# A ring of prompt expert rows cut from three buffers to two, and a table load moved ahead of the late gathers

## The chip, the cores and the metric

The kernel runs on one core of one Trainium2 chip. The metric is the device time of one launch in microseconds; the trace is that of one profiled execution. TensorE does the matrix products, VectorE and ScalarE the elementwise work, GpSimd (POOL in the profile) issues gathers and some loads, and SyncE (SP) streams the weights.

## The reference: two layers of a hybrid backbone

128 context tokens (the prompt) and 512 latent tokens run through two layers. Each layer has four token mixers side by side, a gated merge of them with an output projection, and then an expert layer (PEER). All is float32. What matters here is the expert layer, cut to its core:

```
qry = (hc @ w_query).reshape(-1, PEER_HEADS, 2, PEER_DK // 2)
s = einsum('thpk,hpnk->thpn', qry, sub_keys)          # 8 heads x 2 tables x 128 keys
...                                                    # top 16 of 16 x 16 sums -> e, softmax -> g
act = gelu(einsum('thkd,td->thk', u_tab[e], hc))
y = einsum('thk,thkd->td', g * act, v_tab[e])
```

Each token picks 8 x 16 = 128 experts. For one of these 128 places, the u and v rows of 128 tokens are 128 rows of 2048 floats, 1 MB, fetched by one indirect DMA (a gather). Below, "row i" is the gather of place i for all 128 prompt tokens.

## The kernel before

The prompt's work is one stage ahead of the latent tokens' work, so the prompt's 128 expert rows of layer l are handled while the latent tokens of layer l go through their mixers. Every engine has its own program, written out in order, and they meet at semaphores. For the latent tokens of a layer the order is: projections for convolution and pooling; the query/key stage (16 units of four-chunk projections on TensorE, `L1980`, each with a square on ScalarE, a norm on VectorE, `L1508` to `L1539`, and transposes back on TensorE, `L2019`); pool projections (`L2038`); attention in 48 jobs; the merge stage (32 steps of a gate product `L2129` and a branch product `L2134`); the output and query projections and the scores against the sub-keys; then the latent tokens' own expert rows.

The prompt's rows are spread over this. Rows 0 to 15 (`EARLY = 16`) go with the query/key stage, one to a step: in step n VectorE does the reduction for unit n, the norm of unit n-1, the dot of row n-1 (`L1397`) and the addition of row n-2 to the accumulator (`L1407`). ScalarE makes the weight of a row between its dot and its addition. Rows 16 to 111 go with the merge stage, three to a step, and the rest with the two stages behind it.

GpSimd issues the gathers. The early rows use a ring of three buffers in `arena`; the gather of row i waits until the addition of row i-3 is done (`p_acc`). Behind the sixteenth addition GpSimd issues the loads of the windows of v (`L638`) and the bias loads, which the later two thirds of attention need. Rows 16 and up use a ring of four other buffers (`L664`); they wait for the end of attention (`o_ready`). The latent tokens' sub-keys `sk` (1 MB, `L663`), used by the scores behind the merge stage, are loaded between rows 23 and 24, since the accumulator of the early rows `yacc0` lies in the same place until row 16 is added.

Weights come in chunks of 0.5 MB through a ring of six; a chunk's place is loaded again once TensorE is through with it. In the query/key stage four units use the same four chunks, and they come free during the fourth unit.

The lines that set the order on VectorE in the query/key stage:

```
for n in range(NQ + 1):
    if n < NQ:
        qk_mean(n)
    if n >= 1:
        qk_norm(n - 1)
        prompt_rows(l, (n - 1,))
    ...
prompt_add(l, EARLY - 1)
```

Of the kernel before, what the change touches and what calls it, by code (L numbers as in the profile page):

```python
# [15 lines left out]
D = 1024  # L16
# [19 lines left out]
PAIRS = HEADS * TOPK  # L36
# [197 lines left out]
NP = 4  # L234
EARLY = 16
# [36 lines left out]
def need(eng, s, n):  # L272

    if n > 0:
        eng.wait_ge(s, n)


def backbone(nc, xT, cT, w, ada, small, rowg, lamrow, clay, poolw, subk, rope, edge, mask, bias, ckn, ckd,
             cvn, cvd, experts, y_prompt, y_sample, o_nk, o_nv, o_dk, o_dv):
    with ExitStack() as cx:  # L280
# [3 lines left out]
        def sem(name):  # L284
            return cx.enter_context(nc.semaphore(name))
# [6 lines left out]
        arena = sb("arena", [P, 28800])  # L292
# [20 lines left out]
        peidx = sb("peidx", [P, PAIRS], U32)  # L313
# [3 lines left out]
        def at(tensor, start, *shape):  # L317
            n = int(np.prod(shape))
            v = tensor[:, start:start + n]
            if len(shape) == 1:  # L320
                return v
            names = "abcd"[:len(shape)]
            return v.rearrange(f"p ({' '.join(names)}) -> p {' '.join(names)}", **dict(zip(names, shape)))
# [22 lines left out]
        sk = at(arena, 26752, 16, NKEYS)  # L346
# [10 lines left out]
        def routing(tensor, base):  # L357
# [33 lines left out]
        plamx = at(T, 1280, 2, 64)  # L391

        prow = [at(arena, a, 2 * D) for a in (16512, 18560, 10368, 14464)]
        prow0 = [at(arena, a, 2 * D) for a in (20096, 22144, 24704)]
        yacc0, yacc = at(arena, 27392, D), at(arena, 22656, D)
        pdots, pgel, pwcol = at(T, 2048, PAIRS), at(T, 2176, PAIRS), at(T, 2304, PAIRS)

        w_load = [sem(f"w_load{i}") for i in range(RING)]
# [14 lines left out]
        p_half, p_gate, p_br, p_merged, p_subk = [sem(n) for n in ("p_half", "p_gate", "p_br", "p_merged", "p_subk")]  # L413
        p_idx, p_top, p_gexp, p_gok = sem("p_idx"), sem("p_top"), sem("p_gexp"), sem("p_gok")
        p_row = [sem(f"p_row{i}") for i in range(NP)]
        p_row0 = [sem(f"p_row0{i}") for i in range(3)]
        p_dot, p_w, p_acc = sem("p_dot"), sem("p_w"), sem("p_acc")

        x_ready, sq_ready, root, h_ready = sem("x_ready"), sem("sq_ready"), sem("root"), sem("h_ready")
# [1 line left out]
        ctx_in, subk_in, u_zero, u_ready, conv_done, pool_d = [  # L421
            sem(n) for n in ("ctx_in", "subk_in", "u_zero", "u_ready", "conv_done", "pool_d")]
# [52 lines left out]
                eng.wait_ge(turn[key[0]], TURN[key] + 1)  # L475

        def row_of(i):
            return prow0[i % 3] if i < EARLY else prow[i % NP]

        def weight_of(i):  # L480
            return stp[:, i:i + 1] if i < EARLY else pwcol[:, i:i + 1]
# [4 lines left out]
        def pause(eng):  # L486

            eng.nop(nofuse=True)
# [34 lines left out]
        def _(gp):  # L523
# [77 lines left out]
            for l in range(DEPTH):  # L601
                need(gp, x_ready, l)
                for t in range(NL):
                    gp.tensor_tensor(sq[:, t], x_sb[:, t], x_sb[:, t], ALU.mult).then_inc(sq_ready, 1)
                gp.wait_ge(h_ready, 24 * l + KD)
                pause(gp)
                gp.memset(U, 0.0).then_inc(u_zero, 1)
                own.link(gp.memset(at(bsb, 0, 3, PADDED), 0.0))
                gp.dma_start(dkT[:, :, LAT:TOK], ckd[l]).then_inc(ctx_in, 16)
                gp.dma_start(nkT[:, :, LAT:TOK], ckn[l]).then_inc(ctx_in, 16)  # L610
                gp.dma_start(dv[:, NL, :], cvd[l]).then_inc(ctx_in, 16)
                gp.dma_start(nvc, cvn[l]).then_inc(ctx_in, 16)
                work = [at(bsb, i * PADDED, PADDED) for i in range(3)]
                for g, win in enumerate(POOL_WINDOWS):
                    wait_freed(gp, ("L", l, f"pl{g}"))
                    pause(gp)
                    own.link(gp.tensor_copy(work[0][:, PAD:PAD + LAT], yT[:, g, :]))
                    for means in pool_means(*work, LAT, g, win):
                        pass
                    gp.tensor_tensor(yT[:, g, :], means[:, PAD:PAD + LAT], work[0][:, PAD:PAD + LAT], ALU.subtract).then_inc(pool_d, 1)  # L620
                    gp.wait_ge(pool_d, 4 * l + g + 1)

                for i in range(2):
                    gp.wait_ge(vb_out[i], 32 * (l + 1))
                gp.wait_ge(p_idx, 2 * l + 1)
                for i in range(EARLY):
                    if i >= 3:
                        gp.wait_ge(p_acc, l * PAIRS + i - 2)
                    pause(gp)
                    gp.indirect_dma_start(row_of(i), None, experts,  # L630
                                          bass.IndirectOffsetOnAxis(ap=peidx[:, i:i + 1], axis=0)).then_inc(p_row0[i % 3], 16)
                gp.wait_ge(p_acc, l * PAIRS + EARLY)
                pause(gp)
                vg = vscr.rearrange("(r c) n -> r c n", c=GRID_W)
                for j in range(NJ):
                    for half in range(2):
                        for r in range(4):
                            gp.dma_start(vwin[32 * r:32 * r + 32, 2 * j + half, :],  # L638
                                         vg[4 * half + r, COL0[j]:COL0[j] + KB, :]).then_inc(vb_in, 16)

                for h in range(8):
                    if h >= 2:

                        gp.wait_ge(m_ready, l * NMAPS + MAP0[NDIFF + NL * (h - 1)])
                    pause(gp)
                    bh = at(bsb, (h % 2) * 1024, NJ, ROWS * KB)
                    gp.dma_start(bh, bias[l * 8 + h]).then_inc(bias_in[h % 2], 16)
                    gp.wait_ge(bias_in[h % 2], (l * 4 + (h // 2 + 1)) * 16)
                    pause(gp)
                    for j in range(NJ):  # L650
                        b3 = bh[:, j, :].rearrange("p (r k) -> p r k", k=KB)
                        gp.tensor_tensor(b3, b3, mk[:, j:j + 1, :].broadcast_to([P, ROWS, KB]), ALU.add).then_inc(bias_ok, 1)

                gp.wait_ge(o_ready, NJOBS * (l + 1))
                gp.wait_ge(p_idx, 2 * (l + 1))
                for i in range(EARLY, PAIRS):
                    if i >= EARLY + NP:
                        gp.wait_ge(p_acc, l * PAIRS + i - NP + 1)
                    if i == EARLY + 3:
                        gp.wait_ge(y_diff, 4 * (l + 1))  # L660
                    if i == EARLY + 8:
                        pause(gp)
                        gp.dma_start(sk, subk[l]).then_inc(subk_in, 16)  # L663
                    gp.indirect_dma_start(row_of(i), None, experts,  # L664
                                          bass.IndirectOffsetOnAxis(ap=peidx[:, i:i + 1], axis=0)).then_inc(p_row[i % NP], 16)

                mixer = prompt_mixer(l + 1) if l + 1 < DEPTH else iter(())
                step = None
                for t in range(NL):
                    for i in range(PAIRS):  # L670
                        n = (l * NL + t) * PAIRS + i
                        here = t * PAIRS + i
                        if i % GP == 0:
                            gp.wait_ge(idx_ready, (l * NL + t) * 2 + i // GP + 1)
                        if here == 1:
                            gp.wait_ge(p_acc, PAIRS * (l + 1))
                        if here == 7:
                            wait_unit(gp, ("E", l, "ynP"))
                        if n >= NS:
                            gp.wait_ge(v_done, n - NS + 1)  # L680
                        gp.indirect_dma_start(rows[:, n % NS, :], None, experts,  # L681
                                              bass.IndirectOffsetOnAxis(ap=eidx[:, t % 2, i:i + 1], axis=0)).then_inc(row_in[n % NS], 16)
                        if here == PAIRS:
                            wait_unit(gp, ("C", l, "s15"))
                            step = next(mixer, None)
                        elif step is not None and here >= gather_of(step) + 10:
                            step = next(mixer, None)
                assert step is None and next(mixer, None) is None
# [422 lines left out]
        def _(v):  # L1111
# [274 lines left out]
            def prompt_dot(l, i):  # L1386

                if i < EARLY:
                    v.wait_ge(p_row0[i % 3], (l * ((EARLY + 2 - i % 3) // 3) + i // 3 + 1) * 16)
                else:  # L1390
                    v.wait_ge(p_row[i % NP], (l * ((PAIRS - EARLY) // NP) + (i - EARLY) // NP + 1) * 16)
                if i == 0:
                    for name in ("hna", "hnb"):
                        wait_freed(v, ("P", l, name))
                e = row_of(i)[:, 0:D]
                d = stp[:, i:i + 1] if i < EARLY else pdots[:, i:i + 1]
                v.tensor_tensor_reduce(e, e, htok(NL), 1.0, 0.0, ALU.mult, ALU.add, d).then_inc(p_dot, 1)  # L1397
# [27 lines left out]
            for l in range(DEPTH):  # L1425
# [192 lines left out]
                for s in range(32):  # L1618
                    dp, i, dd = s // 8, s % 8 // 2, s % 2
# [725 lines left out]
```

## Time and profile before

| what | value |
|---|---|
| median of 3 runs | 5128.01 us (5121.45 to 5134.9) |
| profiled execution | 5121.45 us, span 5119.6 us |
| TensorE busy | 4417.8 us, 86% |
| VectorE busy | 3388.3 us, 66% |
| ScalarE busy | 1951.3 us, 38% |
| GpSimd busy | 1661.8 us, 32% |
| HBM read | 1667.33 MB, 327 GB/s over the span |

Busy shares are means over stages that differ: the kernel has stages in which the DMA engines are nearly full and others in which they are idle more than half of the time. A stage has to be read by itself.

### The profile page before, as it was taken

Reading aid. Unit: us, or ns where it says so; the run is one execution under the profiler, and the core shown is the slowest. Engines: PE = TensorE matmul, PEld = TensorE weight load, DVE = VectorE, ACT = ScalarE, POOL = GpSimd, SP = SyncE. Lnnn points to the kernel's source line nnn. Section 1 sums busy time; section 2 is a strip of 40 time slices with the busy share of each in tenths; the row PEclk is TensorE's granted clock in tenths of the full one; section 3 lists DMA queues with packets and bytes.
Section 4 is the critical chain, followed back from the end, with each engine's and each line's share of the span. In section 5 each row is a group of like instructions: output and inputs, shape, how many; then the busy total and the mean of one; then the engine's idle time right before and its main releaser. Section 6 shows DMA issues by size and latency. Waiting matters only on the chain.

```text
span 5119.6 us, 46892 instructions
## 1 busy us (share of the span) xinstructions
PE 4417.8 (86%) x14388; PEld 2284.2 (45%) x14388; DVE 3388.3 (66%) x7266; ACT 1951.3 (38%) x5074; POOL 1661.8 (32%) x1600
## 2 busy tenths in 40 slices
PE   7889888998899888888888898999889987777777
PEld 4674455434645333344544444644464632222222
DVE  4239865777787677775444896777778767576544
ACT  1210543343233434565533035544323433333333
POOL 3003121223244453433332322132224444434332
PEclk8899989999999999999999998999999999999999
DMA  7752526999799999999999143199979999999998
GB/s 286 252 192 79 191 78 249 350 345 351 305 420 420 420 420 411 413 394 418 405 419 419 60 140 124 61 356 356 360 279 420 412 419 422 422 421 419 421 421 353
DMA packets 277115, 1677.27 MB, mean 328 GB/s; under 512 B 31808, under 2 KB 31856, under 8 KB 112384
## 3 DMA queue, kind: packets, MB, share of 16 engines
q0 software_dynamic: 190896, 1365.43, 66.0%
q1 hardware_dynamic: 82944, 302.03, 16.1%
q10 hardware_dynamic: 3024, 6.82, 0.3%
q8 instruction: 115, 1.88, 0.1%
q14 instruction: 136, 1.11, 0.1%
HBM read 1667.33 MB, written 6.82 MB: 327 GB/s over the span
## 4 chain that ended last, share of the span: by engine, by line
DMA 39%; PE 31%; DVE 17%; ACT 7%; issue 5%; POOL 0%; SPq 0%; DVEq 0%; ACTq 0%; POOLq 0%
DMA arena<-experts,bsb 27%; PE ps L2218 12%; DMA arena<-experts,peidx 10%; PE ps L1805 5%; DVE arena L1496 4%; DVE arena L1708 3%; PE ps L1913 2%; PE ps L1980 2%; DMA wring<-w 2%; DVE arena L1407 2%; PE ps L2070 2%; PE ps L2092 2%; PE ps L1781 1%; ACT L1066 1%; ACT T L1070 1%
## 5 line engine op out<-in xcount | busy, mean ns | idle before, releaser
L2218 PE MATMUL ps<-arena,T 128*128 128x512 f32 x4096 | 1967.6, 614 | 445.2 <-ACT T L1070 444.6
L1708 DVE CUSTOM_DVE_ANT_0 arena<-arena,h_sb 128x1024 f32<-128x1024 f32 x1024 | 1252.8, 1227 | 865.0 <-DMA arena<-experts,bsb 861.4
L681 POOL DMA_INDIRECT arena<-experts,bsb x1024 | 1095.8, 1070 | 1741.4 <-PE ps L2218 1582.2
L2218 PEld LDWEIGHTS ps<-arena,T 128*128 128x128 f32 x4096 | 726.1, 192 | 1569.5 <-ACT T L1070 951.7
L1066 ACT ACTIVATE bsb<-T 128x1 f32<-128x1 f32 x1024 | 205.9, 201 | 1303.0 <-DVE T L1708 1301.3
L1805 PE MATMUL ps<-h_sb,wring 128*128 128x256 f32 (+2 forms) x2304 | 517.8, 382 | 35.1 <-DVE h_sb L1447 13.7
L2129 PE MATMUL ps<-h_sb,wring 128*128 128x512 f32 x1024 | 457.6, 600 | 33.5 <-DVE arena L1633 31.0
L1805 PEld LDWEIGHTS ps<-h_sb,wring 128*128 128x128 f32 x2304 | 380.7, 196 | 183.8 <-issue 152.0
L664 POOL DMA_INDIRECT arena<-experts,peidx x224 | 249.5, 1114 | 655.6 <-DVE arena L1407 582.1
L1070 ACT ACTIVATE T<-ident,bsb 128x128 f32<-128x128 f32 x1024 | 410.9, 401 | 33.5
L1397 DVE CUSTOM_DVE_ANT_0 arena<-arena,h_sb 128x1024 f32<-128x1024 f32 x256 | 312.7, 1222 | 113.7 <-DMA arena<-experts,peidx 112.6
L1980 PE MATMUL ps<-wring,h_sb 128*128 128x512 f32 x768 | 338.2, 598 | 0.0
L2129 PEld LDWEIGHTS ps<-h_sb,wring 128*128 128x128 f32 x1024 | 192.6, 191 | 294.3 <-issue 228.1
L1067 ACT ACTIVATE bsb<-bsb,T 128x1 f32<-128x1 f32 x1024 | 301.4, 294 | 33.2
L1407 DVE SCALAR_TENSOR_TENSOR arena<-arena,T 128x1024 f32<-128x1024 f32 x224 | 287.0, 1281 | 0.5 <-ACT T L845 0.5
L2134 PE MATMUL ps<-arena,wring 128*128 128x512 f32 x512 | 230.2, 593 | 0.0
L1980 PEld LDWEIGHTS ps<-wring,h_sb 128*128 128x128 f32 x768 | 146.2, 193 | 175.3 <-issue 175.3
L844 ACT ACTIVATE T<-T 128x1 f32<-128x1 f32 x224 | 45.3, 202 | 444.0 <-DVE T L1397 444.0
L1496 DVE SCALAR_TENSOR_TENSOR arena<-arena,sm 128x512 f32<-128x512 f32 x240 | 184.9, 849 | 0.0
L1805 PE MATMUL ps<-arena,wring 128*128 128x256 f32 (+1 forms) x768 | 150.4, 353 | 25.8 <-DVEq L1639 25.0
L2070 PE MATMUL ps<-arena 64*128 64x128 f32 (+2 forms) x512 | 151.8, 433 | 17.3 <-ACT T L961 15.2
L630 POOL DMA_INDIRECT arena<-experts,peidx x32 | 64.9, 2029 | 284.4 <-DVE arena L1407 171.6
(326 smaller groups left out, 4543.1 us busy)
## 6 DMA issues: line engine op xcount, KB each, us to landing
wring<-w SPq DMA_DIRECT2D x576, 512.0 KB, 6.2
arena<-experts,bsb POOLq DMA_INDIRECT x1024, 15.3
bsb<-bias POOLq DMA_DIRECT2D x16, 512.0 KB, 3.8
arena<-subk POOLq DMA_DIRECT2D x4, 1024.0 KB, 8.3
arena<-experts,peidx POOLq DMA_INDIRECT x256, 8.0
arena<-v_scratch POOLq DMA_DIRECT2D x64, 64.0 KB, 2.0
x_sb<-xT POOLq DMA_DIRECT2D x1, 2048.0 KB, 14.1
v_scratch<-arena ACTq DMA_DIRECT2D x8, 256.0 KB, 2.0
```

The source lines that it names most:

```text
L681: gp.indirect_dma_start(rows[:, n % NS, :], None, experts, bass.IndirectOffsetOnAxis(ap=eidx[:, t % 2, i:i + 1], axis=0)).then_inc(row_in[ ...
L1066: own.link(act.activation(gel[:, i:i + 1], dots[:, t % 2, i:i + 1], ACT.Gelu))
L1067: own.link(act.activation(wcol[:, i:i + 1], gel[:, i:i + 1], ACT.Copy, scale=gate[:, t % 2, i:i + 1]))
L1070: act.activation(diag[:, n % ND, :], ident[:], ACT.Copy, scale=wcol[:, i:i + 1]).then_inc(diag_ok, 1)
L1397: v.tensor_tensor_reduce(e, e, htok(NL), 1.0, 0.0, ALU.mult, ALU.add, d).then_inc(p_dot, 1)
L1407: v.scalar_tensor_tensor(yacc0 if i < EARLY else yacc, row, weight_of(i), yacc0 if i <= EARLY else yacc, ALU.mult, ALU.add).then_inc(p_acc, 1)
L1496: op = v.scalar_tensor_tensor(acc[:, c, :], U[:, c, 1 + k:1 + k + LAT], S(col), acc[:, c, :], ALU.mult, ALU.add)
L1708: v.tensor_tensor_reduce(e, e, htok(t), 1.0, 0.0, ALU.mult, ALU.add, dots[:, t % 2, i:i + 1]).then_inc(dot, 1)
L1805: mm = pe.matmul(bank(key, cols), chunk_of(s, l, c)[:, k * P:(k + 1) * P], src(k), start=(k == 0), stop=(k == KD - 1))
L1980: mm = pe.matmul(bank(key), h_sb[:, t, k, :], chunk_of("L", l, c0 + q)[:, kk * 512:(kk + 1) * 512], start=(k == 0), stop=(k == KD - 1))
L2129: mm = pe.matmul(ps[:, s % 2, :], chunk_of("L", l, c)[:, k * P:(k + 1) * P], h_in(k), start=(k == 0), stop=(k == KD - 1))
L2218: mm = pe.matmul(ps[:, 6 + half, :], diag[:, n % ND, :], rows[:, n % NS, D + half * 512:D + (half + 1) * 512], start=(i == 0), stop=(i == ...
```

## The change

The early ring has two buffers instead of three: the gather of row i waits for the addition of row i-2. The place that comes free takes the early accumulator, so that it no longer lies in the sub-keys' place; and the sub-keys of the latent tokens are loaded right after attention, ahead of row 16's gather, no longer between rows 23 and 24. The semaphores of the ring are numbered to match.

```
-        prow0 = [at(arena, a, 2 * D) for a in (20096, 22144, 24704)]
-        yacc0, yacc = at(arena, 27392, D), at(arena, 22656, D)
+        prow0 = [at(arena, a, 2 * D) for a in (20096, 22144)]
+        yacc0, yacc = at(arena, 25728, D), at(arena, 22656, D)
...
-        p_row0 = [sem(f"p_row0{i}") for i in range(3)]
+        p_row0 = [sem(f"p_row0{i}") for i in range(2)]
...
         def row_of(i):
-            return prow0[i % 3] if i < EARLY else prow[i % NP]
+            return prow0[i % 2] if i < EARLY else prow[i % NP]
...
                 for i in range(EARLY):
-                    if i >= 3:
-                        gp.wait_ge(p_acc, l * PAIRS + i - 2)
+                    if i >= 2:
+                        gp.wait_ge(p_acc, l * PAIRS + i - 1)
                     pause(gp)
...
                 gp.wait_ge(o_ready, NJOBS * (l + 1))
+                pause(gp)
+                gp.dma_start(sk, subk[l]).then_inc(subk_in, 16)
                 gp.wait_ge(p_idx, 2 * (l + 1))
                 for i in range(EARLY, PAIRS):
...
-                    if i == EARLY + 8:
-                        pause(gp)
-                        gp.dma_start(sk, subk[l]).then_inc(subk_in, 16)
...
-                    v.wait_ge(p_row0[i % 3], (l * ((EARLY + 2 - i % 3) // 3) + i // 3 + 1) * 16)
+                    v.wait_ge(p_row0[i % 2], (l * (EARLY // 2) + i // 2 + 1) * 16)
```

## Rows read from the trace of the kernel before

**Rows 1.** The page: chain by line, and the early gathers among the costliest groups.
```profile
DMA arena<-experts,bsb 27%; PE ps L2218 12%; DMA arena<-experts,peidx 10%; PE ps L1805 5%; DVE arena L1496 4%; DVE arena L1708 3%; PE ps L1913 2%; PE ps L1980 2%; DMA wring<-w 2%; DVE arena L1407 2%; PE ps L2070 2%; PE ps L2092 2%; PE ps L1781 1%; ACT L1066 1%; ACT T L1070 1%
...
L630 POOL DMA_INDIRECT arena<-experts,peidx x32 | 64.9, 2029 | 284.4 <-DVE arena L1407 171.6
```

**Rows 2.** Windows: length; PE, PEld, DVE, ACT, POOL busy; PEclk; DMA share; GB/s.
```profile
504.00:640.00 136.00, 120.19 (x315) 55.50 (x313) 112.34 (x204) 68.37 (x113) 32.61 (x16) 0.96 0.51 180
...
930.00:1260.00 330.00, 300.56 (x743) 141.68 (x742) 245.99 (x318) 134.12 (x263) 97.84 (x87) 0.97 0.93 351
```

**Rows 3.** Timeline of POOL, query/key stage of the first layer: start, length, instruction, idle before.
```profile
537.60 0.94 POOL L630 DMA_INDIRECT arena<-experts,peidx  x1 [12.06 <-DVE arena L1404]
548.58 0.94 POOL L630 DMA_INDIRECT arena<-experts,peidx  x1 [10.04 <-DVE arena L1407]
555.88 0.94 POOL L630 DMA_INDIRECT arena<-experts,peidx  x1 [6.37 <-DVE arena L1407]
...
570.49 0.94 POOL L630 DMA_INDIRECT arena<-experts,peidx  x1 [6.36 <-DVE arena L1407]
583.38 0.94 POOL L630 DMA_INDIRECT arena<-experts,peidx  x1 [11.96 <-DVE arena L1407]
590.46 0.94 POOL L630 DMA_INDIRECT arena<-experts,peidx  x1 [6.14 <-DVE arena L1407]
595.16 0.94 POOL L630 DMA_INDIRECT arena<-experts,peidx  x1 [3.76 <-DVE arena L1407]
602.11 0.94 POOL L630 DMA_INDIRECT arena<-experts,peidx  x1 [6.01 <-DVE arena L1407]
609.41 0.94 POOL L630 DMA_INDIRECT arena<-experts,peidx  x1 [6.37 <-DVE arena L1407]
619.42 0.94 POOL L630 DMA_INDIRECT arena<-experts,peidx  x1 [9.07 <-DVE arena L1407]
629.71 0.94 POOL L630 DMA_INDIRECT arena<-experts,peidx  x1 [9.35 <-DVE arena L1407]
634.77 0.94 POOL L630 DMA_INDIRECT arena<-experts,peidx  x1 [4.12 <-DVE arena L1407]
```

**Rows 4.** Timeline of DVE: after an addition, a dot, and attention's first reduction.
```profile
547.72 0.68 DVE L1508 TENSOR_REDUCE st<-T 128x8 f32<-128x512 f32 x1
...
552.68 1.22 DVE L1397 CUSTOM_DVE_ANT_0 arena<-arena,h_sb 128x1024 f32<-128x1024 f32 x1
...
653.92 0.82 DVE L1584 TENSOR_REDUCE st<-ps 128x1 f32<-128x640 f32 x1 [5.64 <-PE ps L2070]
```

**Rows 5.** L630 alone, windows 540 to 650, then 537 to 540, then 629 to 631.
```profile
  DVE arena L1407: 85.9, 12
...
DMA to landing us min/median/max: 5.4/5.6/8.9
...
DMA to landing us min/median/max: 9.0/9.0/9.0
...
DMA to landing us min/median/max: 7.3/7.3/7.3
```

**Rows 6.** Timeline of PE: a unit after a long wait, and one without.
```profile
529.18 1.12 PE L2019 MATMUL ps<-ident,T 128*128 128x128 f32 x4 [10.24 <-DVE T L1539]
530.09 9.14 PE L1980 MATMUL ps<-wring,h_sb 128*128 128x512 f32 x16
...
546.81 7.03 PE L1980 MATMUL ps<-wring,h_sb 128*128 128x512 f32 x16
```

**Rows 7.** Timelines of POOL and DVE around the merge stage's start.
```profile
856.43 1.00 POOL L664 DMA_INDIRECT arena<-experts,peidx  x1 [21.05 <-PE ps L2092]
...
895.91 0.57 POOL L663 DMA_DIRECT2D arena<-subk  x1 [0.95 <-DVE arena L1407]
...
878.33 1.22 DVE L1397 CUSTOM_DVE_ANT_0 arena<-arena,h_sb 128x1024 f32<-128x1024 f32 x1
...
907.30 1.23 DVE L1397 CUSTOM_DVE_ANT_0 arena<-arena,h_sb 128x1024 f32<-128x1024 f32 x1 [4.45 <-DMA arena<-experts,peidx]
```

More of the change, by code:

```diff
@@ L626, in _ @@
                 for i in range(EARLY):
-                    if i >= 3:
-                        gp.wait_ge(p_acc, l * PAIRS + i - 2)
+                    if i >= 2:
+                        gp.wait_ge(p_acc, l * PAIRS + i - 1)
                     pause(gp)
                     gp.indirect_dma_start(row_of(i), None, experts,
-                                          bass.IndirectOffsetOnAxis(ap=peidx[:, i:i + 1], axis=0)).then_inc(p_row0[i % 3], 16)
+                                          bass.IndirectOffsetOnAxis(ap=peidx[:, i:i + 1], axis=0)).then_inc(p_row0[i % 2], 16)
                 gp.wait_ge(p_acc, l * PAIRS + EARLY)
```

## The prediction

> **What bounds the kernel now.** I read the page first, then the windows, then the timelines of GpSimd, VectorE and TensorE around the two places that the diff touches, then the time from issue to landing of single gathers. On the page the reader sees that the chain that ended last is mostly gathers of expert rows, and that the early prompt gathers (L630) do not carry it; it runs through L1980, the projections beside them [rows 1]. So the early rows are now hidden, and the question is by how much. The windows show two different stages: the query/key stage (504 to 640 us) has TensorE busy 120 of 136 us with the DMA engines at 51%, while the merge stage (930 to 1260 us) has them at 93%, 351 GB/s, with TensorE busy 301 of 330 us [rows 2]. In the first stage latency counts, in the second bytes.
>
> In the query/key stage VectorE does, per step, a reduction, the norm of one unit, the dot of row i and the addition of row i-1. The page's idle time of L630, 171.6 us over 24 gathers, is twice the 85.9 us over 12 gathers of the first layer, so the second layer repeats the first [rows 1, 5].
>
> **The early ring, three buffers to two.** Today gather i waits for the addition of row i-3; after the change it waits for that of row i-2. The addition of row i-2 is the last thing in step i-1, and the dot of row i comes in the very next step. The latency, which now spreads over two steps, must fit into one.
>
> Its pieces: an addition ends at 547.72 and the next gather issues at 548.58, 0.86 us [rows 3, 4]. Landing takes 5.4 to 5.6 us from issue where no weights are moving [rows 5]; I take 5.5. From the dot's start (552.68) to the end of the addition behind it is 2.34 us: that addition released the gather at 555.88, less 0.86 is 555.02 [rows 3, 4]. Together one row cannot take less than 0.86 + 5.5 + 2.34 = 8.7 us. Today a row takes 7.30 us in this stage, seen as the distance between gathers, and TensorE's unit and its transposes take the same [rows 3, 6]. With three buffers the latency is spread over two steps and hidden.
>
> Where weights move at the same time (the ring reloads after each fourth unit), landing took 9.0 us at 537.6, 7.3 at 629.7 and up to 8.9 between [rows 5]; such a row takes 0.86 + 9.0 + 2.34 = 12.2 us or, with 7.3, 10.5.
>
> Twelve steps lie between the gathers at 537.60 and 634.77, 97.2 us: 11.0, 7.3, 7.3, 7.3, 12.9, 7.1, 4.7, 6.9, 7.3, 10.0, 10.3, 5.1 [rows 3] (the row at 563.19, between two of 7.3, isn't shown). After the change:
> Steps 2, 3, 6, 7, 9 and 10 are quiet rows: 6 x 8.7 = 52.2.
> Steps 1 and 8 meet the weights: 12.2 + 12.1. Step 1 already waits for TensorE's unit now, and that hides the first part of it.
> Step 4 begins with the reload; between 5.5 and 7.3 I take 6.4, thus 9.6. Step 12 is in the reload, 10.5.
> Steps 5 and 11 hold the convolution's centring and its norm, which keep VectorE and ScalarE busy longer than a gather takes: 12.9 and 10.3 as now.
> Sum 119.8, so 22.6 us more. A thirteenth step stands before the last norm. It waits today for ScalarE, which has the convolution's activation to do first; from the other rows that hold more than the usual work I put it at 9 us, and at the same after: nothing. That puts the end of row 13's addition at 634.77 - 0.86 + 9 = 642.9 now.
>
> Then what is late: the last norm releases TensorE's last transposes, the pool projections and the first scores of attention, all in a row. Row 15 on VectorE is not on that path: its gather waits for row 13's addition, and it is done 8.7 us and one addition of 1.2 us later, 9.9 us behind 642.9, where the first reduction of attention is at 653.92 [rows 4], 11.0 us behind. So its wait is just hidden and I count it at nothing; a gather that meets weights there costs up to 2.4 us. The window loads of v and the bias loads on GpSimd are behind the last early row too; they are needed by the sixteen-jobs-later part of attention, tens of us on, and cost nothing. Attention and all behind it start 22.6 us later, in each layer: +45.2 us. Nothing behind it works ahead of it, since each stage reads what the last one left, so nothing gives it back.
>
> The floor: all landings at 5.4 and no meeting with weights gives nine rows of 8.6, 11.0, 12.9 and 10.3, sum 111.6, +14.4 a layer. The ceiling: 9.0 also in step 4, 12 and 13 gives about +30 a layer.
>
> The Trainium skill (DMA: Bandwidth & Descriptors, "Anatomy of one DMA — SWDGE (gpsimd) path") fits a GpSimd DMA as 2.0 us and bytes over 436 GB/s. For the 1 MB of a gather that is 4.4 us, an estimate from that page, and a quiet row would take 7.6 us and hardly lose anything. The trace does not agree: twelve gathers took 5.4 us at the least [rows 5], and the measurement decides.
>
> **The load of the sub-keys moved ahead of the late gathers.** It is 1.05 MB on GpSimd's own queue. Today it issues at 895.91 with row 24's gather right behind it, and the dot that needs this gather then waits 4.45 us [rows 7]. After the change it issues as soon as attention is over, ahead of rows 16 to 18. Today row 16's gather issues at 856.43 and its dot starts at 878.33, released by VectorE's own order (four reciprocals) and not by a DMA [rows 7], so 3 us of delay to these rows are covered; were they not, the gain would be given back. The merge stage loses 1.05 MB of transfer at 351 GB/s, 3.0 us, and with the DMA at 93% [rows 2] I take it whole: -6.0 us in both layers. The bounds are 0 and the 4.45 us wait, so 0 to -9 us. The extra instruction that lets the load start, and its 0.57 us of issue [rows 7], lie in that cover too. Moving the accumulator and renumbering the semaphores costs nothing: same instructions, same shapes.
>
> **Sum.** +45.2 - 6.0 = +39.2 us. The profiled execution took 5121.45 us (span 5119.6), so 5160.7 by its own time; the median of the runs shown is 5128.01, 6.6 us higher, and with that the forecast is 5167 us.
>
> **The rivals.**
> *Hidden after all.* If a quiet gather lands within the 4.1 us that a 7.3 us step leaves (7.3 - 0.86 - 2.34), the early ring costs nothing and only the -6 us stand: 5122 us. Against it: not one of the twelve landings was under 5.4 [rows 5].
> *The merge stage runs free (the other side).* The prompt gathers of the merge stage fall behind TensorE. If the missing load lets them keep up and TensorE never waits there, the stage is shortened by 330 - 301 = 29 us a layer [rows 2], 58 in all: 45 - 58 = -13 us, 5115 us. It decides only if nearly the whole 29 us follow from that one load. Against it: the DMA engines are at 93% long after the load is through.
> *The clock falls.* The new waits make TensorE idle 1.4 us or more in every step. After 10.24 us of idling the unit took 9.14 us where others take 7.03 [rows 6], 2.1 us more, and unit and transposes at 9.4 would be longer than the quiet row of 8.7: +0.7 in some eight steps, 11 us over both layers, 5178 us. If the engine never came back to its upper level in this stage, units near twice 7.03 us and their transposes would set steps of about 14 us: some 5 us more in eight steps, 80 us in all, 5247 us. For it: the granted clock of the stage is 0.96 as it is, so it does fall at gaps. Against it: most new gaps are a fifth of a step, and even 88% busy holds 0.96 [rows 2]. The Trainium skill (TensorE: Matmul & The Clock Gate, "HAM oscillation — how this bites in real kernels") describes such waits for data between short bursts of matmuls as throttling the engine each time; that is this rival's longer form, and the trace so far bears out only the shorter.
> *The move does nothing.* If the merge stage's pace comes from latency and not from bytes, -6 becomes 0 and the time 5173; this is inside my range.
>
> **How the numbers follow.** Forecast with its bounds 84%, hidden 6%, merge stage free 3%, clock 7%. The range: +28.8 - 9 = +20 us at the low end, +60 - 0 at the high end, thus 5148 to 5188 us. Most of the clock rival's short form is inside. A measurement of this kernel tells about 0.3%, 15 us, from no change: slower by more holds the forecast and the clock, 90% after taking off a little for the floor; within it 7%; faster 3%.
>
> **What the new profile should show.** In the query/key stage the dots of the early rows (L1397) wait for their gathers, 1 to 5 us each, in some ten of the steps, where none waits now; gathers stand 8.7 us apart in quiet steps; TensorE's transposes (L2019) wait for the norm. Attention begins 23 us later than now. In merge the dot of row 24 waits about 1 to 2 us and not 4.45, and the stage is 3 us shorter. What would make me wrong: landings that are shorter because fewer gathers are in flight, an overlap with the weights that shifts as the steps stretch, or a lower granted clock in the 140 us of the stage.

## The result, and the profile after

The change makes the kernel slower. The changed kernel takes 5172.76 us in the median (5168.32 to 5182.8, four runs), the kernel before 5129.7 us (5121.45 to 5134.9, four runs): 43 us more, ratio 1.0083 with a 95% interval of 1.0062 to 1.0103. The forecast was 5167 us in a range of 5148 to 5188. The profiled execution after has a span of 5162.9 us, 43.3 us over that of before.

The lines behind 664 have moved up by one in the changed kernel: `L1397`, the dot, is `L1396` there, `L1407` is `L1406`, and the sub-keys' load is `L656`.

The page after, its chain by line:

```profile
DMA arena<-experts,bsb 26%; DMA arena<-experts,peidx 13%; PE ps L2217 13%; PE ps L1804 5%; DVE arena L1495 4%; DVE arena L1707 3%; DVE arena L1406 2%; PE ps L1912 2%; DMA wring<-w 2%; PE ps L2069 2%; PE ps L2091 2%; PE ps L1780 1%; ACT T L1069 1%; ACT L1065 1%; ACT bsb L1066 1%
```

The share of the prompt's gathers in the chain went from 10% [rows 1] to 13%, and `L1980`, the projections of the query/key stage, is gone from this list. Within the first layer's query/key stage alone, the chain was 46% `L1980` before; after, 51% of it is gathers and none of it is these projections.

To place the time, I take the first instruction of four groups in each layer as marks: the first transposes of the query/key stage, the first scores of attention, the first gate product of the merge stage, the first product of the latent tokens' experts. The stretches between them, in us, from the two profiled executions:

| stretch | before, layers 1 and 2 | after, layers 1 and 2 | more |
|---|---|---|---|
| start to the first transposes | 529.2 | 522.6 | -6.6 |
| query/key stage to attention | 123.4, 123.0 | 146.5, 144.1 | +23.1, +21.2 |
| attention to merge | 209.3, 166.2 | 218.4, 162.9 | +9.1, -3.3 |
| merge to latent experts | 491.0, 489.4 | 485.9, 492.3 | -5.0, +3.0 |
| latent experts | 1665.2, 1323.0 | 1665.3, 1324.8 | +0.1, +1.7 |

The two query/key stages took 44.3 us more, against 43.3 in all: they hold the whole of it. The other stretches also differ between executions of kernels that do the same in them: in the eight profiles of the experiments below the first layer's attention took between 207.6 and 238.6 us, and up to the first transposes it took 524.9 to 528.2 us.

The early gathers after, timeline of GpSimd in the first layer:

```profile
531.03 0.94 POOL L630 DMA_INDIRECT arena<-experts,peidx  x1 [13.30 <-DVE arena L1403]
544.12 0.94 POOL L630 DMA_INDIRECT arena<-experts,peidx  x1 [12.16 <-DVE arena L1406]
552.96 0.94 POOL L630 DMA_INDIRECT arena<-experts,peidx  x1 [7.90 <-DVE arena L1406]
561.46 0.94 POOL L630 DMA_INDIRECT arena<-experts,peidx  x1 [7.56 <-DVE arena L1406]
...
609.99 0.94 POOL L630 DMA_INDIRECT arena<-experts,peidx  x1 [8.90 <-DVE arena L1406]
618.56 0.94 POOL L630 DMA_INDIRECT arena<-experts,peidx  x1 [7.64 <-DVE arena L1406]
...
646.09 0.94 POOL L630 DMA_INDIRECT arena<-experts,peidx  x1 [7.73 <-DVE arena L1406]
657.85 0.94 POOL L630 DMA_INDIRECT arena<-experts,peidx  x1 [10.82 <-DVE arena L1406]
```

Where the gathers stood 7.30 us apart [rows 3], they now stand 8.5 to 8.8 us apart. The dots (`L1396`) of the same stage, what they waited for, and the two timelines' rows of one dot each:

```profile
its engine sat idle before it (us, times) until:
  DMA arena<-experts,peidx: 37.4, 12
```

```profile
558.26 1.22 DVE L1396 CUSTOM_DVE_ANT_0 arena<-arena,h_sb 128x1024 f32<-128x1024 f32 x1 [1.33 <-DMA arena<-experts,peidx]
...
606.78 1.23 DVE L1396 CUSTOM_DVE_ANT_0 arena<-arena,h_sb 128x1024 f32<-128x1024 f32 x1 [5.05 <-DMA arena<-experts,peidx]
```

No dot waited for a gather in this stage before; now twelve of sixteen do, 37.4 us in all. More is waited for than is lost, since one wait took another's place: VectorE waited 17.2 us for ScalarE's squares of TensorE's units in this stage before, and 7.2 us now.

At the end of the stage there is a wait that I had not foreseen. ScalarE's timeline and TensorE's:

```profile
665.96 0.20 ACT L843 ACTIVATE stp<-stp 128x1 f32<-128x1 f32 x1 [5.51 <-DVE stp L1396]
666.19 0.29 ACT L844 ACTIVATE stp<-stp,pgate 128x1 f32<-128x1 f32 x1
666.39 2.40 ACT L953 ACTIVATE arena<-ps,sm 128x512 f32<-128x512 f32 x4
```

```profile
658.69 1.12 PE L2018 MATMUL ps<-ident,T 128*128 128x128 f32 x4 [9.29 <-DVE T L1525]
659.60 5.93 PE L2037 MATMUL ps<-arena,pw_sb 128*128 128x512 f32 x8
669.11 2.51 PE L2069 MATMUL ps<-arena 64*128 64x512 f32 x8 [3.58 <-ACT arena L953]
```

ScalarE makes the weight of row 15 (`L843`), whose dot is late, before it evacuates the pool projections (`L953`); TensorE needs the evacuations before its first scores (`L2069`) and waits 3.58 us.

The moved load, timelines of GpSimd and VectorE at the merge stage:

```profile
882.38 0.56 POOL L656 DMA_DIRECT2D arena<-subk  x1 [23.86 <-PE ps L2091]
883.24 1.01 POOL L663 DMA_INDIRECT arena<-experts,peidx  x1 [0.31 <-issue]
```

```profile
904.00 1.21 DVE L1396 CUSTOM_DVE_ANT_0 arena<-arena,h_sb 128x1024 f32<-128x1024 f32 x1
...
928.23 1.23 DVE L1396 CUSTOM_DVE_ANT_0 arena<-arena,h_sb 128x1024 f32<-128x1024 f32 x1 [2.00 <-DMA arena<-experts,peidx]
```

The load is out of the way: row 16's dot at 904.00 waits for no DMA, and row 24's dot waits 2.00 us and not 4.45 [rows 7]. Yet the stretch from merge to the latent experts is shorter in one layer and longer in the other (-5.0 and +3.0).

### The profile page after: what moved, and what is told of

Read it like the earlier page. It is cut to its first block, busy times and chain, and to the rows that moved or that the text cites. A ratio compares the mean times of both kernels' runs of the same rounds, so it can differ in the third digit from the quotient of the medians.

```text
span 5162.9 us, 46892 instructions
## 1 busy us (share of the span) xinstructions
PE 4427.5 (86%) x14388; PEld 2284.0 (44%) x14388; DVE 3387.4 (66%) x7266; ACT 1951.4 (38%) x5074; POOL 1663.2 (32%) x1600
## 4 chain that ended last, share of the span: by engine, by line
DMA 42%; PE 29%; DVE 17%; ACT 6%; issue 6%; POOL 0%; SPq 0%; DVEq 0%; ACTq 0%; POOLq 0%
DMA arena<-experts,bsb 26%; DMA arena<-experts,peidx 13%; PE ps L2217 13%; PE ps L1804 5%; DVE arena L1495 4%; DVE arena L1707 3%; DVE arena L1406 2%; PE ps L1912 2%; DMA wring<-w 2%; PE ps L2069 2%; PE ps L2091 2%; PE ps L1780 1%; ACT T L1069 1%; ACT L1065 1%; ACT bsb L1066 1%
## 5 line engine op out<-in xcount | busy, mean ns | idle before, releaser
L1396 DVE CUSTOM_DVE_ANT_0 arena<-arena,h_sb 128x1024 f32<-128x1024 f32 x256 | 312.6, 1222 | 186.8 <-DMA arena<-experts,peidx 185.5
L1406 DVE SCALAR_TENSOR_TENSOR arena<-arena,T 128x1024 f32<-128x1024 f32 x224 | 286.7, 1280 | 0.1
L843 ACT ACTIVATE T<-T 128x1 f32<-128x1 f32 x224 | 45.3, 202 | 442.6 <-DVE T L1396 442.6
L630 POOL DMA_INDIRECT arena<-experts,peidx x32 | 65.6, 2048 | 342.2 <-DVE arena L1406 228.3
L2069 PE MATMUL ps<-arena 64*128 64x128 f32 (+2 forms) x512 | 150.2, 435 | 22.4 <-ACT T L960 16.8
## 6 DMA issues: line engine op xcount, KB each, us to landing
arena<-subk POOLq DMA_DIRECT2D x4, 1024.0 KB, 10.6
```

Source lines behind the costliest of these rows:

```text
L1406: v.scalar_tensor_tensor(yacc0 if i < EARLY else yacc, row, weight_of(i), yacc0 if i <= EARLY else yacc, ALU.mult, ALU.add).then_inc(p_acc, 1)
```

## The experiments

My theory after the result: the ring of two costs the whole of it, since the round trip from an addition over the gather to the next dot must fit into one step; the moved load gives something back that is too small to see in one pair of traces. The rivals: the moved load or the moved accumulator costs the time; two gathers at a time cannot keep up in whatever order; and, for the load, that bytes do not set the merge stage's pace at all.

**Only the ring.**

```
-        prow0 = [at(arena, a, 2 * D) for a in (20096, 22144, 24704)]
+        prow0 = [at(arena, a, 2 * D) for a in (20096, 22144)]
...
-                    if i >= 3:
-                        gp.wait_ge(p_acc, l * PAIRS + i - 2)
+                    if i >= 2:
+                        gp.wait_ge(p_acc, l * PAIRS + i - 1)
```

> The kernel before with the early ring cut to two buffers, and nothing else: the sub-keys' load stays between rows 23 and 24, the accumulator stays where it was. My theory (the ring costs the time, the load gives a little back): the distance from the first transposes of the query/key stage to the first scores of attention grows from 123 us to 144 to 147 us in both layers, and the time is about 44 us over before, 5170 to 5180 us, ratio 1.008 to 1.010. If the moved load is worth its forecast 6 us, this kernel is 6 us slower than the changed kernel; the rival, that the load is worth nothing, has them equal. A rival for the loss, that it comes from the moved load or the moved accumulator, has this kernel at the time of before.

Measured: 5174.78 us, ratio 1.0091 (1.0075 to 1.0106). The stage, in the windows of both layers (length; PE, PEld, DVE, ACT, POOL busy; granted clock; DMA share; GB/s):

```profile
524.90:670.20 145.30, 117.44 (x296) 54.41 (x296) 96.02 (x167) 73.68 (x123) 13.11 (x14) 0.90 0.46 160
3047.60:3195.50 147.90, 119.69 (x298) 55.13 (x298) 96.00 (x167) 73.72 (x123) 13.19 (x15) 0.89 0.45 157
```

The ring alone gives the whole loss: the stages are 145.3 and 147.9 us, the second a little over the forecast 144 to 147. The time is 2 us from the changed kernel's, inside both intervals, so whether the load is worth 6 us or nothing is not told by it.

**Only the load.**

```
-        mrow = [at(arena, 16512, 2, 512), at(arena, 24704, 2, 512)]
+        mrow = [at(arena, 16512, 2, 512), at(arena, 27392, 2, 512)]
...
-        prow0 = [at(arena, a, 2 * D) for a in (20096, 22144, 24704)]
-        yacc0, yacc = at(arena, 27392, D), at(arena, 22656, D)
+        prow0 = [at(arena, a, 2 * D) for a in (20096, 22144, 26368)]
+        yacc0, yacc = at(arena, 25344, D), at(arena, 22656, D)
...
                 gp.wait_ge(o_ready, NJOBS * (l + 1))
+                pause(gp)
+                gp.dma_start(sk, subk[l]).then_inc(subk_in, 16)
...
-                    if i == EARLY + 8:
-                        pause(gp)
-                        gp.dma_start(sk, subk[l]).then_inc(subk_in, 16)
```

> The sub-keys' load moved ahead of row 16 as in the change, with the early ring kept at three buffers; to make the room, the third buffer, the accumulator and the second layer's modulation rows take other places in the same arena. My theory: the query/key stage stays at 123 us, the dot of row 24 waits about 1 to 2 us and not 4.45, the merge stage and what follows it up to the latent experts is 3 us shorter in each layer, the time 0 to 9 us under before, ratio 0.998 to 1.000. The rival: transfers that leave the merge stage do not speed it up, since its pace is set by the round trip of the ring of four, ratio 1.000 and stage lengths that differ by no more than they do between two executions.

Measured: 5122.96 us, ratio 0.9991 (0.9977 to 1.0005). The query/key stages are 123.6 and 122.1 us, so the moved load and the moved accumulator cost nothing there. The merge stage from its first gate product to its last gating product is 363.4 and 363.7 us, where before it was 365.2 and 361.2. The interval takes in both the rival (nothing) and my -6 us (ratio 0.9988), so the time decides between them not at all; the stage lengths lean to the rival's side. Over the profiled kernels with a ring of four and one load, this stage is 361.2 to 366.2 us, mean 364.0, with the load at row 24 (four stages), and 357.9 to 366.9, mean 362.9, with it ahead of row 16 (eight stages): about 1 us, less than the spread.

**The tail: ScalarE's order.** The changed kernel, with row 15's weight behind the evacuations.

```
                         qk_out(n - 2)
-                        prompt_weights(l, (n - 2,))
+                        if n < NQ + 1:
+                            prompt_weights(l, (n - 2,))
...
+                prompt_weights(l, (EARLY - 1,))
```

> The changed kernel, but ScalarE makes the weight of early row 15 behind the four evacuations of the pool projections and not ahead of them. The changed kernel's trace shows TensorE waiting 3.58 us for these evacuations, which stand behind row 15's late dot. My theory: this wait falls back to about 1 us, the stage from the first transposes to the first scores goes from 146.5 and 144.1 to about 144 and 142 us, some 5 us off the total. The rival: VectorE, busy with row 15 until then, is as late, and attention's first reduction starts no sooner, so nothing is gained.

Measured: 5168.9 us, ratio 1.0071 (1.0052 to 1.0091). TensorE's timeline at the first scores, of the first and of the second layer:

```profile
671.11 1.36 PE L2071 MATMUL ps<-arena 64*128 64x512 f32 x8 [1.03 <-issue]
...
3211.96 1.36 PE L2071 MATMUL ps<-arena 64*128 64x512 f32 x8 [1.03 <-issue]
```

The wait is gone in both layers (3.58 and 2.01 us in the changed kernel, 2.4 and 1.98 in the run with the ring alone). The stages are 144.2 and 143.6 us, against a mean of 146.0 over the four stages of the changed kernel and the ring alone (144.1 to 147.9): 2 us a layer. The piece that the edit touches says the same: from the issue of row 15's gather to the first scores it is 8.6 and 7.3 us here, against 9.9 to 11.3 in those four. So about a tenth of the loss is this queue on ScalarE. The total moves by less than its interval.

**The order within the step.** The changed kernel, two buffers, with the addition ahead of the dot.

```
                         qk_norm(n - 1)
-                        prompt_rows(l, (n - 1,))
+                        if n >= 2:
+                            prompt_add(l, n - 2)
+                        prompt_dot(l, n - 1)
```

> The changed kernel with two buffers, but in each step of the query/key stage VectorE adds row i-1 before it takes the dot of row i, so that the next gather is released ahead of the wait for the present one. My theory (the loss is the round trip from an addition to the next dot, which must fit into one step): the round trip 0.86 + 5.5 us now has the dot of the row between it and a whole step of 7.3 us to run in, the dots wait for no quiet gather, the stage returns to 123 to 128 us in both layers, and the time to 5121 to 5135 us, 38 to 45 us under the changed kernel. The rival, that two gathers at a time cannot keep up whatever the order (bytes or GpSimd's issue), has the stage stay above 140 us. A smaller rival: the addition then waits for ScalarE's weight, about 1 us in the later steps.

Measured: 5128.5 us, ratio 0.9999 (0.9988 to 1.001), 44 us under the changed kernel. Timelines of VectorE and GpSimd in the first layer, and the windows of both stages:

```profile
550.56 1.28 DVE L1406 SCALAR_TENSOR_TENSOR arena<-arena,stp 128x1024 f32<-128x1024 f32 x1
551.75 1.22 DVE L1396 CUSTOM_DVE_ANT_0 arena<-arena,h_sb 128x1024 f32<-128x1024 f32 x1
...
557.86 1.28 DVE L1406 SCALAR_TENSOR_TENSOR arena<-arena,stp 128x1024 f32<-128x1024 f32 x1
559.06 1.22 DVE L1396 CUSTOM_DVE_ANT_0 arena<-arena,h_sb 128x1024 f32<-128x1024 f32 x1
```

```profile
552.61 1.18 POOL L630 DMA_INDIRECT arena<-experts,peidx  x1 [6.13 <-DVE arena L1406]
559.91 1.17 POOL L630 DMA_INDIRECT arena<-experts,peidx  x1 [6.13 <-DVE arena L1406]
```

```profile
527.00:652.10 125.10, 112.78 (x298) 52.97 (x298) 96.43 (x167) 73.61 (x123) 17.06 (x16) 0.94 0.53 186
3015.60:3140.20 124.60, 112.72 (x297) 52.92 (x297) 96.72 (x167) 73.68 (x123) 16.64 (x16) 0.94 0.53 187
```

This settles the mechanism. Two buffers, the same gathers, the same bytes: the gathers stand 7.30 us apart again, since the gather issued at 552.61 is wanted by the dot at 559.06, 6.45 us later, and lands in time, after 5.8 us. Only the dot moved from inside the round trip to outside it. In the first layer five dots still waited for gathers, 11.1 us in all, and in the second four, 7.6 us. The smaller rival shows too: six additions of the first layer waited for ScalarE's weight, 3.3 us together. That these waits are why the stages are 125.1 and 124.6 us and not 123 is likely and not shown. It was not that two gathers in flight are too few for the DMA engines.

**More loads in the merge stage.** The kernel before, the load five times.

```
-                    if i == EARLY + 8:
+                    if i in (EARLY + 8, EARLY + 24, EARLY + 40, EARLY + 56, EARLY + 72):
+                        if i > EARLY + 8:
+                            gp.wait_ge(subk_in, 16 * (5 * l + (i - EARLY - 8) // 16))
...
-                        pe.wait_ge(subk_in, 16 * (l + 1))
+                        pe.wait_ge(subk_in, 80 * (l + 1))
```

> The kernel before with the sub-keys' load issued five times a layer in the merge stage and not once, at rows 24, 40, 56, 72 and 88 (the same table into the same place). It doubles, and more, the cost under dispute. If bytes set the pace of this stage, as I forecast, each load costs 1.05 MB at 340 GB/s, 3.1 us: four more are 12.3 us a layer, the length from the first gate product to the last gating product goes from about 363 to 375 us in both layers, 25 us in all, ratio 1.005. If the stage has slack between its gathers that takes up a load, as the run with the load moved away suggests (about 1 us), it is 1 us a load, 367 us, 8 us in all, ratio 1.0015. If a load costs only the wait it makes at its own place, the dots behind it wait 2 to 3 us longer and the rows after them catch up.

Measured: 5142.75 us, ratio 1.0025 (1.0011 to 1.0039). The merge stage is 374.8 and 371.5 us, 373.2 in the mean, 9.2 over the 364.0 of the kernels with one load at row 24: 2.3 us for each load. That is between the two forecasts, nearer to bytes. The third forecast, that the rows behind catch up, fails with it. The time agrees with the stages: 18 us more by them, 6 to 20 us by the interval. By itself this would have spoken for my bytes; the next run shows that the DMA engines had room. What is left as an explanation is that a load on GpSimd's queue stands ahead of the gather behind it and delays a ring that has no slack, and that this costs about as much as its bytes would; no run shows that apart.

**A fifth buffer in the merge stage.** Three early buffers; rows 16 to 111 go round five buffers, the fifth in the sub-keys' place; the sub-keys are loaded between rows 113 and 114.

```
+SLOT = {i: (0, 1, 2, 4, 3)[(i - EARLY) % 5] if i < 112 else (1, 2, 3, 0)[(i - 112) % 4] for i in range(EARLY, PAIRS)}
...
-        prow = [at(arena, a, 2 * D) for a in (16512, 18560, 10368, 14464)]
+        prow = [at(arena, a, 2 * D) for a in (16512, 18560, 10368, 14464, 26752)]
...
-                    if i >= EARLY + NP:
-                        gp.wait_ge(p_acc, l * PAIRS + i - NP + 1)
+                    if PREV[i] is not None:
+                        gp.wait_ge(p_acc, l * PAIRS + PREV[i] + 1)
```

> Three early buffers, and a ring of five in place of four for the merge stage's rows 16 to 111; the fifth takes the sub-keys' place, and the sub-keys are loaded between rows 113 and 114, behind the merge stage. If the merge stage's pace is set by bytes, the length from the first gate product to the last gating product stays at 361 to 366 us and the dots still wait some 44 us for gathers in it. If it is set by the round trip of a ring of four, the waits fall by half or more and the stage comes down toward TensorE's own 32 steps of 10.3 us and its start and end, about 345 us, 18 us a layer, time about 5095 us, ratio 0.993. The late load of the sub-keys could make the first scores wait: not seen if it lands within the 8 output projections behind it.

> The ring of five again, same kernel as the run before: 5063 us, ratio 0.986, the stretch from the first gate product to the last gating product 330 us in both layers with TensorE busy throughout. It is run again because two of its six times were far above the others; if these belong to the kernel and not to the chip's moment they come again.

Measured: 5063.03 us, ratio 0.9859 (0.9841 to 0.9877), and the second time 5061.92 us, ratio 0.9864 (0.9835 to 0.9892). Two of the first six times, 7455 and 15530 us, lie far outside and did not come back in the four of the second run (5054 to 5073 us). The windows of the merge stage: first layer of the kernel before, then both layers of the changed kernel, then the first layer of this one, second time:

```profile
861.90:1227.10 365.20, 337.31 (x768) 144.77 (x768) 274.22 (x340) 149.48 (x282) 106.42 (x94) 0.99 0.90 340
...
887.50:1247.90 360.40, 334.86 (x768) 144.18 (x768) 274.26 (x340) 149.53 (x282) 105.32 (x93) 0.99 0.91 344
3345.80:3711.00 365.20, 338.06 (x768) 145.38 (x768) 273.87 (x340) 149.42 (x282) 105.92 (x93) 0.98 0.91 340
```

```profile
857.90:1187.80 329.90, 329.84 (x768) 145.81 (x768) 271.07 (x340) 149.82 (x283) 123.62 (x93) 1.00 0.95 372
```

The same 768 matmuls take 329.9 us instead of 360 to 365, and TensorE has no gap left in them. My expectation of 345 us was too long: I had added a start and an end to the 32 steps of 10.3 us, and the stage is those 32 steps alone. The gathers of this stage, time to landing of the kernel before (932 to 1215 us) and of this one (930 to 1176 us):

```profile
DMA to landing us min/median/max: 5.9/8.0/11.0
```

```profile
DMA to landing us min/median/max: 6.5/9.2/12.5
```

A gather takes longer to land, 9.2 us against 8.0 in the median, and yet the stage is shorter, because five are on their way instead of four. The DMA engines went from 340 to 372 GB/s: what had looked full at a share of 0.90 was not. The page of the kernel before already had a sign of it, which I did not use: its row of GB/s over 40 slices of the execution.

```profile
GB/s 286 252 192 79 191 78 249 350 345 351 305 420 420 420 420 411 413 394 418 405 419 419 60 140 124 61 356 356 360 279 420 412 419 422 422 421 419 421 421 353
```

The merge stage is the 350, 345, 351 there. The latent tokens' expert rows, which come through a ring of eight buffers, run at 411 to 422 in most of their slices. The dots' waits for gathers in the stage fell from 46.4 us over 43 dots to 11.6 over 12.

**Only the late load.** The kernel before, with its one load between rows 113 and 114.

```
-                    if i == EARLY + 8:
+                    if i == 114:
```

> The kernel before with the ring of four and three early buffers, and only the sub-keys' load moved to where the ring of five has it, between rows 113 and 114. It tells the two edits of the ring of five apart. If the fifth buffer made the gain, this kernel has the merge stretch at 361 to 366 us with some 44 us of waits for gathers, and the time is 5120 to 5135 us, ratio 0.998 to 1.000. If the late load made it, the stretch is near 330 us.

Measured: 5130.23 us, ratio 0.9998 (0.9981 to 1.0016). The merge stage is 363.0 and 362.7 us, and the dots wait in it as before; in the first layer it is:

```profile
  DMA arena<-experts,peidx: 44.2, 47
```

So the fifth buffer makes the gain. Within the merge stage the place of the load, early, middle or late, moves the mean by about 1 us. Behind it the late load is not free: from the last gating product to the first product of the latent experts it is 132.5 and 132.9 us here, against 125.6 to 128.5 in the kernels with the load early or in the middle, some 5 us a layer by these two stretches, though the median time, no more than 8 us over the kernel before by its interval, does not show it. The ring of five, with the same late load, takes 129.6 to 130.9 us there, so it gives back about 3 of its 33 us. The version with five buffers beats both kernels: 1.4% under the kernel before, 110 us under the changed one.

## Why the prediction was right, and where it was not

**The early ring, +45.2 us: right in mechanism; that the sum is so close is in part luck.** The ring alone shows the loss, and the order within the step takes it away again with two buffers. The period of a quiet row was put at 8.7 us and came out at 8.5 to 8.8. Where a gather sets the step, the sum 0.86 + landing + 2.34 holds to 0.03 us: a landing of 5.27 us went with a step of 8.50, one of 8.53 with 11.76. (I had taken the start of the instruction behind the addition, 547.72, for its end, 547.80; that moves 0.08 us from one piece to the other and leaves the sum.)

The sizes of the terms missed both ways. In the first layer the twelve steps took 646.09 - 531.03 = 115.1 us, where I had 119.8: +17.9 and not +22.6. Steps 4, 8 and 12, which I had meeting the weights, took 8.5, 9.8 and 8.7 us where I had 9.6, 12.1 and 10.5, while step 1 took 13.1 and not 12.2. In the second layer they took 117.2 us, up from 96.9, and there step 8 did meet the weights: 12.8 us, with a landing of 9.5. So which gathers meet a reload shifts as the steps stretch, and it differs between the layers, which I had taken as alike. Two terms that I had put at nothing, below, filled the gap, and the stages came to +23.1 and +21.2 us where I had +22.6 each.

**"A thirteenth step ... at the same after: nothing": wrong in the first layer.** Before, it took the 9 us that I had put. After, it took 11.8, 2.8 more, since its dot waited 5.95 us for a gather that landed 8.5 us after its issue. In the second layer the same gather landed in 5.3 us and the step took 8.6. The ring alone has 10.6 and 11.0. What I called free hangs on whether this gather meets the weights.

**"Its wait is just hidden": wrong.** I had looked at what VectorE does behind the last norm and not at ScalarE's queue, where the weight of row 15 stands ahead of the evacuations that the first scores need. It costs 2 us a layer by the run that moves it.

**The moved load, -6.0 us: not borne out; the stage lengths say about -2 us, which is not told from nothing.** The step that failed is "in the second bytes": I took a DMA share of 93% and 351 GB/s for a limit, and the fifth buffer took the stage to 372 GB/s. The move did what I said at its own place, row 24's wait fell from 4.45 to 2.00 us, but the rows behind it were bound by the round trip of a ring of four, and that the move leaves as it was. Why a load costs 2.3 us when four are added and about 1 us when the one is moved away is not settled; the second number is within the spread of the stages. With this term at nothing the forecast would have been 5173 us, where 5172.76 was measured; that, too, is closer than its terms deserve.

**The rivals.** "Hidden after all" is refuted by 37.4 us of waits. "The clock falls" happened in its small form and cost nothing that shows: the granted clock of the stage went from 0.94 to 0.88 in the first layer, and after a wait of 4.53 us one unit took 9.57 us where others take 7.03. VectorE was held up by a gather meanwhile, and its reduction of that unit started at 590.91, right behind the late addition and without a wait of its own; after the other such unit, at 635.27, it waited 0.20 us. TensorE's timeline of the changed kernel:

```profile
579.77 1.11 PE L2018 MATMUL ps<-ident,T 128*128 128x128 f32 x4 [4.53 <-DVE T L1538]
580.68 9.57 PE L1979 MATMUL ps<-wring,h_sb 128*128 128x512 f32 x16
590.09 0.60 PE L2018 MATMUL ps<-ident,T 128*128 128x128 f32 x4
590.52 7.03 PE L1979 MATMUL ps<-wring,h_sb 128*128 128x512 f32 x16
```

The next unit takes 7.03 us again. "The merge stage runs free" did not come from the moved load, and I was right that one load would not do it. But my reason against it, the DMA share, was false: with a fifth buffer the stage does run free, 330 us where it was 363, and the 33 us a layer are near the 29 us that this rival read from TensorE's idle time in a window of the stage [rows 2].

The Trainium skill (Perfetto Trace Analysis, "Identifying the Most-Contended Engine") says that the occupancy of the 16 DMA engines misleads and that HBM utilization is to be read instead; the runs here agree, as a share of 0.90 at 340 GB/s left room for 372 GB/s. The same page ("Optimization Strategy") of the Trainium skill says that one gap coming again and again on the engine that should be saturated can mean too few buffers. The merge stage is such a case: 43 of the 93 dots up to its last gating product waited, TensorE was busy 337 of 365 us, and with one buffer more it was busy throughout.

## What to carry to other kernels

Before a ring is made smaller, add up the round trip from the release of a buffer to the use of what is loaded into it, and compare it with the time between the two in program order: if it fits only with a buffer more, look first whether the release can be moved ahead of the wait. A high DMA share in a stage whose transfers are issued by a ring is no proof that bytes set the pace; one more buffer is the test. When a piece of work becomes late, look at every engine's queue for what stands behind it, not only at the engine that does it.

## What was new about the hardware

Gathers of 1 MB, each 128 rows of 8 KB, landed in 5.2 us at the least from issue, in 8.0 us (median) with four in a ring beside the weights, and in 9.2 us with five, while the throughput of the stage rose from 340 to 372 GB/s. With the fifth on its way each took longer to land and yet more landed in the same time, at a DMA share that was 0.90 before and 0.95 after. A direct load of 1 MB put among the gathers of a ring of four cost the stage 2.3 us each, by a run with four added.
